# Differential attention in a two-block transformer kernel: joining the two heads' probabilities before they are turned, and normalising straight from PSUM

## The reference, cut to what matters

```python
def differential_attention(q1, q2, k1, k2, v, lam):
    # (softmax(q1 k1^T) - lam * softmax(q2 k2^T)) v, causal. v: (B, S, H, 2*Dh)
    ...
        a = causal_block_probs(q1b, k1, start) - lam * causal_block_probs(q2b, k2, start)
        return jnp.einsum('bhqk,bkhd->bqhd', a.astype(v.dtype), v)
...
    o = differential_attention(q[:, :, :, 0], q[:, :, :, 1], k[:, :, :, 0], k[:, :, :, 1], v, lam)
    o = rms_norm(o, subln_g, SUBLN_EPS) * (1.0 - lam_init)
    return o.reshape(b, s, DIFF_V) @ w_out
```

## Time and profile before

| | |
|---|---|
| median of 3 executions | 1428.4 us (1427.56 to 1449.4) |
| the profiled execution | 1427.14 us |
| its span, first to last instruction | 1425.1 us |
| mean granted TensorE clock | 0.973 of full speed |
| busy: PE, DVE, ACT, POOL | 91%, 47%, 39%, 2% |
| bytes moved by DMA | 336.83 MB |
| differential attention stage | 420.1 to 454.6 us of the span |

### The profile page before, as it was taken

One profiled execution on the slowest core, in us unless ns is written; L12 is line 12 of the kernel. 1 busy time (PEld: TensorE's weight loads), 2 busy tenths in 40 slices (PEclk: granted clock), 3 DMA queues, 4 the chain that ended last, 5 costly groups with the idle time before them and its releaser, 6 DMA issues.

```text
span 1425.1 us, 19426 instructions
## 1 busy us (share of the span) xinstructions
PE 1303.9 (91%) x7252; PEld 938.3 (66%) x7252; DVE 674.9 (47%) x1399; ACT 550.8 (39%) x1072; POOL 32.6 (2%) x68
## 2 busy tenths in 40 slices
PE   7999899999998899999889799998879978999886
PEld 5877899997877799998777534333267864343322
DVE  6657666666768666556566511110056562111102
ACT  5355544456445554445474211110055531111101
POOL 0000000000001000000100000000000000000000
PEclk9999999999999999999899899999999798999998
DMA  8531455554540455555314599999963095999996
GB/s 338 178 117 66 150 190 186 177 177 148 191 162 1 154 175 188 190 188 192 127 60 171 225 400 410 409 409 409 410 245 103 12 372 224 409 409 410 409 409 253
DMA packets 92188, 336.83 MB, mean 236 GB/s; under 512 B 10512, under 2 KB 10640, under 8 KB 91984
## 3 DMA queue, kind: packets, MB, share of 16 engines
q1 hardware_dynamic: 92016, 335.51, 63.9%
q0 software_dynamic: 96, 0.30, 0.1%
HBM read 334.72 MB, written 1.05 MB: 236 GB/s over the span
## 4 chain that ended last, share of the span: by engine, by line
PE 70%; DMA 12%; DVE 7%; ACT 5%; SPq 3%; issue 2%; POOL 1%; DVEq 0%; ACTq 0%; POOLq 0%
PE bank L1307 14%; PE bank L1309 14%; PE bank L1308 14%; DMA expert_part<-stream 12%; PE bank L1581 9%; PE bank L1609 5%; SPq L350 3%; PE bank L1426 2%; PE bank L1535 2%; DVE w_low L766 2%; PE bank L1434 1%; ACT tok L448 1%; ACT w_high L438 1%; PE bank L1370 1%; PE bank L1383 1%
## 5 line engine op out<-in xcount | busy, mean ns | idle before, releaser
L766 DVE TENSOR_TENSOR w_low<-raw,w_high 128x1024 fp32r<-128x1024 f32 (+1 forms) x246 | 285.5, 1213 | 129.2 <-ACT w_high L438 129.0
L1581 PE MATMUL bank<-expert_part,slots_x 128*64 128x512 f32 x1024 | 235.5, 596 | 29.0 <-DMA expert_part<-stream 27.7
L438 ACT ACTIVATE w_high<-raw 128x1024 fp32r<-128x1024 f32 (+1 forms) x246 | 241.8, 1044 | 45.1 <-PE bank L1309 44.7
L1307 PE MATMUL bank<-x_high,w_high 128*128 128x256 f32 (+1 forms) x712 | 201.8, 283 | 4.2 <-DVE x_low L785 4.0
L1309 PE MATMUL bank<-x_high,w_low 128*128 128x256 f32 (+1 forms) x712 | 201.3, 283 | 0.0
L1308 PE MATMUL bank<-x_low,w_high 128*128 128x256 f32 (+1 forms) x712 | 201.3, 283 | 0.0
L1581 PEld LDWEIGHTS bank<-expert_part,slots_x 128*64 128x64 f32 x1024 | 74.2, 136 | 184.8 <-issue 183.0
L1075 DVE SCALAR_TENSOR_TENSOR rope_a<-rope_a,combine,bank 128x256 f32<-128x256 f32 x32 | 15.4, 481 | 327.6 <-ACT rope_a L591 327.6
L1307 PE MATMUL bank<-w_high,x_high 128*128 128x512 f32 (+1 forms) x416 | 163.6, 393 | 4.2 <-DVE x_low L785 2.3
L1308 PE MATMUL bank<-w_low,x_high 128*128 128x512 f32 (+1 forms) x416 | 161.4, 388 | 0.0
L1309 PE MATMUL bank<-w_high,x_low 128*128 128x512 f32 (+1 forms) x416 | 161.2, 388 | 0.0
(11 more groups left out here) (247 smaller groups left out, 1611.3 us busy)
## 6 DMA issues: line engine op xcount, KB each, us to landing
expert_part<-stream SPq DMA_DIRECT2D x384, 512.0 KB, 15.2
raw<-stream SPq DMA_DIRECT2D x244, 512.0 KB, 5.0
const_sb<-const SPq DMA_DIRECT2D x1, 2070.0 KB, 13.7
residual<-x SPq DMA_DIRECT2D x2, 512.0 KB, 4.2
final_gain<-fgain SPq DMA_DIRECT2D x2, 512.0 KB, 14.8
out<-residual SPq DMA_DIRECT2D x2, 512.0 KB, 2.6
small_sb<-small SPq DMA_DIRECT2D x1, 765.0 KB, 6.2
rope_a<-router POOLq DMA_DIRECT2D x2, 144.0 KB, 4.6
```

The costliest lines, as they stand in the source:

```text
L438: nc.scalar.activation(wh[:, u, cols], raw[:, u, cols], ACT.Copy).then_inc(w_high, 1)
L766: tt(wl[:, u, cols], raw[:, u, cols], wh[:, u, cols].bitcast(F32), ALU.subtract).then_inc(w_low, 1)
L1307: mm(o, ah, bh, start=start, stop=False, **kw)
L1581: ins = mm(B[0][half * CAP:(half + 1) * CAP, :], xg[p // 4 % 2][:, k, x_of], w[:, at:at + 512], start=k == 0, stop=k == KT - 1)
```

## The change

The stage gets its own code on all engines (`diff_attention` on VectorE and TensorE, `diff_exps` and `head_squares` on ScalarE, a longer loop on GpSimd) and works on a pair j of heads at a time. After the exponentials, VectorE takes the reciprocals of both heads' sums; GpSimd multiplies the second head's probabilities by its reciprocal and by minus lambda; VectorE joins them with the first head's (`join`). Only the joined probabilities are turned and multiplied by `v`. ScalarE squares the PSUM result, and VectorE writes `tok` from PSUM with the head norm in one instruction. The scores use four banks and the probabilities four buffers. The general `attention` loses its differential branches and is otherwise the same.

```diff
+        diff_probs = [probs[:, 0, :], probs[:, 1, :], zm[:, 0, :], zm[:, 1, :]]
+        token_cols = ((0, 0, P), (1, P, 3 * P))
...
@@ GpSimd
-            for j in range(8):
+            pool.wait_ge(rden_ready, 1)
+            for j in range(-1, 8):
+                if j + 1 < 8:
+                    a = 2 * (j + 1) + 1
+                    pool.wait_ge(rden_ready, j + 2)
+                    for t, lo, hi in token_cols:
+                        p2 = diff_probs[a % 4][:, lo:hi]
+                        ins = nc.gpsimd.tensor_scalar(p2, p2, rden[:, a, t:t + 1], lamb[:, 6:7], ALU.mult, ALU.mult)
+                    ins.then_inc(second_scaled, 1)
+                if j < 0:
+                    continue
                 pool.wait_ge(hss_ready, j + 1)
                 cols = slice(2 * j, 2 * j + 2)
                 link(nc.gpsimd.tensor_scalar(msq[:, cols], hss[:, cols], 1.0 / P, SUB_EPS, ALU.mult, ALU.add))
...
@@ ScalarE
+            def diff_exps(j):
+                for a in (2 * j, 2 * j + 1):
+                    act.wait_ge(nm_ready, 16 + a + 1)
+                    if j >= 2:
+                        act.wait_ge(p_tr, 16 + 2 * (j - 1))
...
+            def head_squares(j):
+                act.wait_ge(pv_done, 16 + 2 * j + 2)
+                for t in range(NT):
+                    ins = nc.scalar.activation((rope_a, rope_b)[j // 4][:, t, (j % 4) * P:(j % 4 + 1) * P],
+                                               B[4 + j % 2][:, t * P:(t + 1) * P], ACT.Square,
...
-            softmaxes(16, range(2, 16), head_squares)
-            head_squares(17)
+            for j in range(-1, 9):
+                if j + 2 < 8:
+                    diff_exps(j + 2)
+                if 0 <= j - 1:
+                    head_squares(j - 1)
...
@@ VectorE, inside the new diff_attention
+                def scores(j):
+                    for a in (2 * j, 2 * j + 1):
+                        dve.wait_ge(s_done, first + a + 1)
+                        if a >= 2:
+                            dve.wait_ge(p_ready, first + a - 1)
...
+                def join(j):
+                    dve.wait_ge(rden_ready, j + 1)
+                    dve.wait_ge(second_scaled, j + 1)
+                    p1, p2 = diff_probs[2 * j % 4], diff_probs[(2 * j + 1) % 4]
+                    for t, lo, hi in token_cols:
+                        ins = stt(p1[:, lo:hi], p1[:, lo:hi], rden[:, 2 * j, t:t + 1], p2[:, lo:hi], ALU.mult, ALU.add)
+                    ins.then_inc(probs_joined, 1)
...
+                def outputs(j):
                     dve.wait_ge(hrs_ready, j + 1)
...
+                    z = B[4 + j % 2][:, 0:2 * P].rearrange("p (t d) -> p t d", t=NT)
+                    tt(tok[:, :, j * P:(j + 1) * P], z, hrs[:, 2 * j:2 * j + 2].unsqueeze(2).broadcast_to([P, NT, P]), ALU.mult)\
...
+                def rest():
+                    for j in range(-1, 10):
+                        if j + 2 < 8:
+                            scores(j + 2)
+                        if j + 1 < 8:
+                            reciprocals(j + 1)
+                        if 0 <= j - 2:
+                            outputs(j - 2)
+                        if 0 <= j < 8:
+                            turned(j)
+                        if j + 1 < 8:
+                            join(j + 1)
...
@@ TensorE, inside the new diff_attention
+                    for lo, hi, t in ((0, 128, 0), (128, 384, 1)):
+                        for a in (2 * j, 2 * j + 1):
...
+                def turn(j):
+                    pe.wait_ge(probs_joined, j + 1)
...
+                def rest():
+                    scores(1)
+                    for j in range(-1, 8):
+                        if j + 3 < 8:
+                            scores(j + 3)
+                        if j >= 0:
+                            values(j)
+                        if j + 1 < 8:
+                            turn(j + 1)
```

More of the change, by code:

```diff
@@ L509, in projections @@
                         qkT_copy(n, (qT, kT)[(g - 1) % 2], 4 * ((g - 1) // 2))
-                    if g == 5:
+                    if g == 5 and first:
+                        diff_exps(0)
+                    elif g == 5:
                         softmaxes(first, (0, 1))
@@ L814, in scaled, with attention @@
                     ins.then_inc(qk_tok_ready, 1)
-            def attention(first, n, masks, scale, dv, diff, between=None, score_bank=0, turned_bank=6):
+            def attention(first, n, masks, scale, dv, between=None, score_bank=0, turned_bank=6):
                 def scores(a):
@@ L845, in outputs @@
                     dve.wait_ge(pv_done, first + a + 1)
-                    if diff and a % 2:
-                        dve.wait_ge(o_done, first + a)
                     for t in range(NT):
                         z = B[4 + a % 2][:, t * dv:(t + 1) * dv]
-                        col = (a // 2 if diff else a) * dv
-                        o = tok[:, t, col:col + dv]
-                        if diff and a % 2:
-                            ins = stt(o, z, rden[:, a, t:t + 1], o, ALU.mult, ALU.add)
-                        else:
-                            ins = ts(o, z, rden[:, a, t:t + 1], None, ALU.mult)
+                        ins = ts(tok[:, t, a * dv:(a + 1) * dv], z, rden[:, a, t:t + 1], None, ALU.mult)
                     ins.then_inc(o_done, 1)
@@ L1170, in kinds1 @@
                 rope(n, c, banks, *(("cos_q", "sin_q"), ("cos_k", "sin_k"))[g % 2])
[L1172 removed]
+            start, rest = attention(0, 16, lambda a: cs("dilated") if a < 8 else forget_mask[a - 8], 1.0, HD)
             projections(C_HYB, 0, kinds0, start, forget_masks)
@@ L1189, in _ @@
             link(ts(lamb[:, 6:7], lamb[:, 5:6], -LAM_INIT, None, ALU.add))
-            start, rest = attention(16, 16, lambda a: cs("causal"), 1.0, P, True, head_norms)
+            start, rest = diff_attention()
             projections(C_DIFF, 4, kinds1, start)
             rest()
-            head_norms(17)
             low(T_L1O, xl, xh, lambda k: gain_sub[:, 0:1])
@@ L1460, in rest, with diff_attention, scores, values @@
                         values(a)
+                return start, rest
+            def diff_attention():
+                first = 16
+                def scores(j):
+                    if j >= 2:
+                        pe.wait_ge(nm_ready, first + 2 * (j - 1))
+                    for lo, hi, t in ((0, 128, 0), (128, 384, 1)):
+                        for a in (2 * j, 2 * j + 1):
+                            q, k = head_rows(a)
+                            ins = mm(B[a % 4][:, lo:hi], q[:, t * P:(t + 1) * P], k[:, 0:hi - lo], start=True, stop=True)
+                            if t:
+                                ins.then_inc(s_done, 1)
+                def turn(j):
+                    pe.wait_ge(probs_joined, j + 1)
+                    if j >= 2:
+                        pe.wait_ge(pT_ready, first + 2 * (j - 1))
+                    for i in range(3):
+                        ins = nc.tensor.transpose(B[6 + j % 2][:, i * P:(i + 1) * P], diff_probs[2 * j % 4][:, i * P:(i + 1) * P],
+                                                  ident)
+                    ins.then_inc(p_tr, 2)
+                def values(j):
+                    pe.wait_ge(pT_ready, first + 2 * j + 2)
+                    if j >= 2:
+                        pe.wait_ge(o_done, first + 2 * (j - 1))
+                    z, pt = B[4 + j % 2], prT[:, j % 2, :]
+                    of_head = [v[:, t, j * P:(j + 1) * P] for t in range(NT)]
+                    mm(z[:, 0:P], pt[:, 0:P], of_head[0], start=True, stop=True)
+                    mm(z[:, P:2 * P], pt[:, P:2 * P], of_head[0], start=True, stop=False)
+                    mm(z[:, P:2 * P], pt[:, 2 * P:3 * P], of_head[1], start=False, stop=True).then_inc(pv_done, 2)
+                def start():
+                    scores(0)
+                def rest():
[7 more added lines that the diff above has]
+                            turn(j + 1)
                 return start, rest
@@ L1725, in _ @@
             normed_transposes(T_L1)
-            start, rest = attention(16, 16, head_rows, lambda a, t: v[:, t, (a // 2) * P:(a // 2 + 1) * P], P)
+            start, rest = diff_attention()
             projections(C_DIFF, 4, T_L1, start)
```

52 lines of the change are left out of this document (29 added, 23 removed).

## The result

The changed kernel takes longer by 1.02%: the ratio to the kernel before is 1.0102, 95% interval 1.0088 to 1.0116, from six executions of each, which is 14.5 us on a median of 1428 (13 to 17 by the interval). Its profiled execution took 1443.21 us, the one before 1427.14: 16.1 more. The forecast was 1440, with 1433 to 1447 around it, so the profiled time lies inside and 1442.5 (1428 times the ratio) does too. To read the times here one must know that two of the six executions before and three of the six after took 20 to 26 us longer than the rest, and that the ratios leave these out. The three that count for the changed kernel took 1440.87, 1441.82 and 1443.21 us, so the profiled one is the longest of them.

What follows compares the result with a forecast made beforehand. The prediction took the stage to be bound by a closed circle of waits through GpSimd, ScalarE and VectorE, 6.0 us a turn. 9.5 + 2.3 + 0.7 = 12.5 us on 1427.14 gave 1439.6, forecast as 1440, range 1433 to 1447.

Steps and rivals of the forecast that it cites:

- The sum: Whole kernel: 9.5 us for the stage, 2.3 for slower clock, 0.7 behind the stage, together 12.5 us more.
- its two terms: The stage: 9.5 us more at TensorE's full clock, and 2.3 us more for the fallen clock.
- TensorE's and VectorE's work: In the stage, per pair: TensorE 2.0 us instead of 4.0, VectorE 2.6; every engine under 2.7 on throughput alone.
- The circle: Waits through GpSimd, ScalarE and VectorE, from one join back to the next, set each turn: 4.9 us + X, 6.0 in all.
- X: GpSimd's scaling of the second head's probabilities, two multiplications 128 and 256 wide: taken as 1.1 us, between 0.6 and 2.0.
- The begin: Start of the stage, from TensorE's resuming to pair 1's join: 7.2 us.
- the five turns: Pairs 2 to 6 in the stage, five turns of the circle: 30.0 us at full clock.
- The tail and the last step: End of the stage: pair 7 takes 2.1 us, then transposes to output and release 4.7 us.
- The clock: TensorE in the stage falls to 1.2 GHz within two or three turns; a slow turn costs 0.3 us more.
- the clock holding: Rival: TensorE stays at 2.4 GHz in the stage, giving 1437 us, or 1433 with X at 0.6; chance 0.23.
- the dear scaling: Rival: GpSimd's X is 2.0 us or more, each 1 us costing about 8; 1447 us at 2.0; chance 0.10.
- the open circle: Rival: norm factors come early, VectorE's 2.7 us per pair counts, giving 1421 us; chance 0.07 together with nothing to see.

Runs made afterwards that it cites:

- e7: Changed kernel without scaling on GpSimd (joined as p1 + q p2, q from VectorE) and with ScalarE's squares issued ahead of the exponentials; ratio to before 0.9984.
- e1: Changed kernel with GpSimd issuing the scaling of pair j + 2 ahead of the norm factor of pair j; ratio to before 0.9986.
- e2: Changed kernel with ScalarE issuing the squares of pair j ahead of the exponentials of pair j + 3; one execution 1427.52 us.
- e3: Changed kernel with GpSimd doing each pair's power twice, the first into a spare tile; one execution 1445.83 us.
- e4: Changed kernel with GpSimd scaling only 128 of the second head's 384 columns, part of the computation left out; one execution 1439.76 us.
- e5: Changed kernel with idle identity transposes on TensorE ahead of each pair's wait for the join and its values; 1445.88 us.
- e6: Changed kernel without scaling on GpSimd: joined as p1 + q p2, q from VectorE, missing factor put into squares and norm factor; ratio to before 0.9994.

## Why the prediction was right, point by point

- **The sum** was 2 us short: it gave 12.5, the timed difference is 14.5. By its own terms it ends at 1439.6 + 1.3 = 1440.9 and not 1440. In the profile the stage took 1 us more than its two terms, what was added behind it came out 0.5 smaller, and some 3 us lie elsewhere, for which the sum had no term.
- **Where the change acts** held: this stage accounts for 12.8 of the 16.2 us between the spans. The rest is below.
- **TensorE's and VectorE's work** held. Two pairs' scores, sixteen instructions, took 1.58 us, which for two pairs is 0.79 each, below the 0.86 that the sum took and the 0.93 of the earlier trace rows (here no end is counted between them). Where nothing makes it wait, VectorE turns a pair in 2.6 to 2.8 us (e7). "In under 2.7 us" was the right bound for the change with a free circle.
- **The circle** held, link by link. The sum was 4.9 + X, measured 5.00 + 0.98. The join to the next start was 0.67 and not 0.56; from there to the exponentials 0.78 and not 0.68, with the transposes of TensorE as the last to be waited for; squares 0.60 and not 0.70. No run here separates the two paths, scores and transposes, by which this link is closed. e1 and e2 each open one link and get the turn down to 3.1 to 3.4 us; e3 and e4 lengthen and shorten the circle and move the turn by what they add and take.
- **X**, the largest unknown, was put at 1.1 between 0.6 and 2.0 and measured 0.98 for the two. (The prediction prices an X of 1.32 at 1.3 us more; by its own 8 us for each 1 us of X it is 1.8.) The Trainium skill ("GPSIMD Engine Reference", section "Engine selection") gives its factor of two for operations with two input tensors and calls those with one roughly line rate; the scaling has one tensor, so the prediction weighed it against the wrong half of that sentence. One by one the scalings take 0.45 and 0.56 us, VectorE's joins of the same widths 0.35 and 0.48 from start to end, though VectorE issues its two in 0.67 and GpSimd takes 0.98. No one-tensor operation of these widths runs on VectorE here. Against the join the trace stands nearer to the page so read than to a factor of two.
- **The begin** was 7.35 us to where pair 1's join lets the next instruction start (7.2 predicted), the five turns 30.8 (31.5, with the slow clock counted in; 30.0 at full clock).
- **The tail and the last step** were too short in the sum. Pair 7's join came 2.64 us after pair 6's, not 2.1, and from the end of pair 7's join it took 6.5 us, where 4.7 and 0.95 for the clock had been laid out. The timelines of TensorE and VectorE show what was missed:

```profile
457.48 0.90 PE L1546 MATMUL bank<-const_sb,probs 128*128 128x128 f32 x3 [2.71 <-DVE probs L918]
458.83 0.56 DVE L925 COPY probs<-bank 128x384 f32<-128x384 f32 x1 [1.01 <-issue]
459.31 0.74 DVE L918 SCALAR_TENSOR_TENSOR stick_z<-stick_z,rden 128x128 f32<-128x128 f32 x2
460.46 0.63 PE L1558 MATMUL bank<-v,probs 128*128 128x128 f32 x2
460.89 0.85 PE L1546 MATMUL bank<-const_sb,stick_z 128*128 128x128 f32 x3
```

  The scaling of pair 7 was done at 458.61, but pair 6's copy stood ahead of its join. It waited for transposes that took 0.90 at 1.2 GHz, and began 0.45 us after they had ended; the profile doesn't name what that was for. In e5, where the same transposes took 0.55, the two joins stood 2.27 apart. Then pair 7's transposes stood behind pair 6's values, still at 1.2 GHz, and began at 460.89, 0.8 us after the join's end at 460.0. The prediction laid out the end with every other engine free; at half the clock TensorE isn't. These two places (0.5 and 0.85 us) more than make up the 1 us by which the stage (12.8) went over its two terms, 9.5 and 2.3.
- **The clock** fell in the second turn (432.9), as forecast, came back once for 3.4 us, fell again and stayed, and a slow turn cost 0.35 us (0.3 forecast). That it was priced small was right: e5 has a turn of 5.97 at full clock. The path was the one that the prediction named, the transposes ahead of the exponentials.
- **Behind the stage** 0.7 us were added for the longer slow stretch. It was about 0.2: the first operation of the next norm stands 12.1 us later than before (491.03 instead of 478.90), where the stage's end stood 11.9 later.
- **What the sum didn't have**: about 3.4 us of the profiled difference lie outside the stage, none of it in work that the change touches. TensorE reached the stage 0.9 us earlier, and behind the stage the difference goes from 12.1 to 16.2 us, not evenly: the norm operations that stood at 478.90, 674.89, 696.47, 787.66 and 818.04 before come 12.1, 13.4, 12.9, 17.8 and 16.6 us later. Slow stretches of the clock stand at other places: windows of the kernel before, then of the one after,

```profile
125.00:130.00 5.00, 5.00 (x26) 4.50 (x25) 3.50 (x8) 4.03 (x9) 0.00 (x0) 0.80 0.01 3
```
```profile
125.00:130.00 5.00, 5.00 (x26) 4.15 (x25) 4.07 (x9) 4.49 (x10) 0.00 (x0) 1.00 0.01 3
...
495.00:500.00 5.00, 3.06 (x17) 2.85 (x18) 3.88 (x10) 3.67 (x9) 0.00 (x0) 0.77 0.00 0
```

  The dip at 123.6 of before isn't in after; after has one at 497.7 and a longer one later, 17.1 us from 767.4, where before had 13.7 from 799.4. By their places these two make the step up to 17.8 and the one back to 16.6. Whether the change causes them, by moving the later code, or they are a matter of the single execution, no run here separates. The timed difference (14.5) lies between the stage's own 12.8 and the profiled 16.1, so some of it was this execution.

The rivals: the clock holding was wrong in this profile; the dear scaling was wrong (0.98); the open circle was wrong for the kernel as it stands, but e1, e2 and e7 show what it would have been, 1421 forecast and 1424 to 1428 measured. What stood between is seen in their rows: in e1 the join still waits 0.40 us for the scaling of its own pair, in e2 mostly 0.41 to 0.67, and in both the tail runs at half the clock; in e7, where no join waits, the stage is 27.3 us, and the prediction's 2.7 a pair had given 27.9.

## What to carry to other kernels

When a change moves work onto an engine that is nearly idle, don't count its busy time; follow its queue. Write down for each engine which instruction stands ahead of the new one and for whom that one waits, and if the path comes back to the new work's own consumer, add up the loop: its length is the turn, whatever the engines' loads are. And try the same work at another place of the queue before giving it up: here one exchange of order took 47.3 us to 32.4.

## What the runs showed of the hardware

**The clock can stay low through a whole attention, though TensorE is busy.** In e7's profiled execution, TensorE ran at 1.2 GHz from 94.6 to 149.2, in e6's from 94.3 to 149.0, in code that none of the experiments touches. Windows of e7, of e6, then of e1, over the same times:

```profile
95.00:149.00 54.00, 53.14 (x201) 43.12 (x202) 26.05 (x116) 15.06 (x59) 0.00 (x0) 0.50 0.01 3
```
```profile
95.00:149.00 54.00, 53.14 (x201) 43.00 (x201) 25.81 (x116) 14.70 (x59) 0.00 (x0) 0.50 0.01 3
```
```profile
95.00:149.00 54.00, 51.29 (x297) 41.59 (x296) 37.15 (x132) 25.02 (x77) 0.86 (x2) 1.00 0.18 61
```

TensorE was busy for 53.14 of 54 us at 1.2 GHz and got no faster: 201 instructions where e1 did 297. These two executions took 1442.62 and 1449.02 us, where the medians of e7 and e6 are 1423.53 and 1427.78: 19 and 21 us more. Ahead of it stood, in e7's timeline of TensorE, a wait of 1.18 us, and the first scores behind it still ran at full speed:

```profile
92.32 0.55 PE L1494 MATMUL bank<-const_sb,probs 128*128 128x128 f32 x3 [1.18 <-ACT v L479]
92.80 0.92 PE L1486 MATMUL bank<-kT,qT 64*128 64x128 f32 x4
...
94.84 1.65 PE L1486 MATMUL bank<-kT,qT 64*128 64x128 f32 x4
```

The same wait of 1.18 us stands there in all ten traces, so it doesn't explain why the clock fell in these two. What does is open.

**GpSimd's price is more in the instruction than in the columns.** A multiplication by two scalars from memory took 0.45 us at 128 columns (e4) and 0.54 to 0.56 at 256 (0.99 less 0.45, and the mean duration in the changed kernel's trace). From these two widths alone that is about 0.35 us fixed and 0.7 to 0.85 ns a column. The slope that the earlier trace rows suggested, 1.5 ns, was about twice too steep.

**Scores of two heads on different row halves of TensorE go side by side**, in longer runs too: sixteen instructions of four heads in 1.58 us, where one head's four take 0.85 to the next start, which would be 3.4 for four heads. The Trainium skill ("TensorEngine Tiling (Array Packing)", section "Key Properties") says that different tiles of the array can load weights and multiply in parallel; the trace agrees, 0.79 us for two heads' eight.
